# Half-height score operands replaced by zero-padded 128-row operands in the gated cell, the block attention and the sparse branches

## Chip, cores and metric

The kernel runs on 1 core of one Trainium2 chip. The metric is the device time of one execution in microseconds. TensorE is called PE here, VectorE DVE, ScalarE ACT and GpSimd POOL.

## The reference

Two transformer blocks for one sequence of 256 tokens with a width of 1024, all in float32. What matters for this change are the places in which heads of 64 channels meet in a product:

```
# gated cell (4 heads of 64): q.k weighted by exp(decays), chunkwise
w = exp(dlog - m_t) * einsum('bhtd,bhsd->bhts', q, k)
# block attention (4 heads of 64; one block of 256 keys here), relative bias, causal
s_own = einsum('bhqd,bhkd->bhqk', qc, k_own) * 64**-0.5 + bias
# sparse branches (8 query heads of 64, 2 key groups, rotary): compressed keys (15),
# selected keys and window keys; with 256 tokens all 256 keys are seen in the last two
out = g_cmp * attend(q, k_cmp) + g_slc * attend(q, k_slc) + g_win * attend(q, k_win)
```

Between and after them stand a recurrent cell with 64-channel decays, cross attention with 128-channel heads, two feed-forward parts, a forgetting attention and a table of 16384 experts.

## The kernel before

All weights come from DRAM as 450 pieces of 512 KB, through four buffers (SP issues the loads). ACT rounds each piece to a high half (`round_piece`, line 1143), DVE makes the low half (`remainder`, line 1575), and PE multiplies them as three products (`mm3`, lines 535, 538 and 539). `feed(key)` on ACT and DVE prepares the pieces of the slot after `key`. Results in the ring of four PSUM banks are ordered by one list, `jobs()`: each job waits until the job four before it has been copied out.

The products of this change are not split in halves. They are float32 matmuls, and one of them shows as two MATMUL rows in the trace. Three places have them.

The gated cell (`mlstm_unit`, units 0 to 2). Each unit makes the decays with a selector of 4 rows (`mD`, line 789) and the query-key products with 64 rows (`mQK`, line 797). Heads 0 and 2 lie in partitions 0 to 63 of their tiles, heads 1 and 3 in partitions 64 to 127. Between the first half's heads and the second half's, `fence(ins)` lets PE wait until its own last matmul is complete. Unit 0 runs before input slot 12, and units 1 and 2 between slots 12 and 13.

The block attention (`ATT1`, 3 units) makes its scores in `score(u)`, line 684, in the same manner, with a fence in each unit, among the projections of the memory.

The last attention (`ATT3`, 22 units) has 6 units of forgetting attention (line 688, whole tiles of 128 rows, whose other half holds zeros and the decays), then 4 units over compressed keys, 6 over selected keys and 6 over window keys (line 696, 64 rows: heads 0 to 3 use partitions 0 to 63, heads 4 to 7 partitions 64 to 127, so that all heads of a unit use the same half, without a fence). An iteration of `attention` on PE is: scores of unit i, in most iterations one half of a merge projection (`merge_half`, lines 535, 538, 539 into `acc`), the transposes of unit i-1 (`turn`, line 705), and the value products of unit i-2 (`pv`, line 730; those of the compressed units have 15 rows).

Around them, ACT copies the projections with their bias into SBUF (`input_copy`, lines 1243 and 1244), and DVE turns the queries and keys of the sparse branches by their rotary angles (`roped`, lines 1921 to 1923). POOL waits until the first feed-forward part is done, clears halves of the forgetting attention's tile (lines 1510 and 1511), and puts the decays in (lines 1519 to 1528).

Of the kernel before, what the change touches and what calls it, by code (L numbers as in the profile page):

```python
# [18 lines left out]
P = 128  # L19
T = 256  # L20
# [246 lines left out]
def build(nc, a):  # L267

    with ExitStack() as ctx:
# [84 lines left out]
        t1 = pl.take(18 * T).rearrange("p (k t) -> p k t", k=18)  # L354
        TT = {name: t1[:, 2 * i:2 * i + 2, :] for i, (name, _) in enumerate(T1)}
# [13 lines left out]
        hm = pl.take(NT * GW).rearrange("p (t n) -> p t n", t=NT)  # L369
        ho = pl.take(NT * GW).rearrange("p (t n) -> p t n", t=NT)  # L370
# [21 lines left out]
        nqT, kkT = t2[:, 0:4], t2[:, 4:6]  # L392
# [112 lines left out]
        def _(pe):  # L505
# [164 lines left out]
            def score(u):  # L670
# [6 lines left out]
                for i in EVEN_ODD[len(heads)]:  # L677
                    h = heads[i]
                    if i == 1 and kind == "moba":
                        fence(ins)  # L680
                    o = b[:, i * n:(i + 1) * n]
                    r = slice((h % 2) * HD, (h % 2) * HD + HD)
                    if kind == "moba":
                        ins = mm(o, TT["aq"][r, h // 2, tok], TT["ak"][r, h // 2, 0:n], start=True, stop=True)
                    elif kind == "cross":
                        ins = mm(o, cqT[:, h, tok], ckT[:, h, :], start=True, stop=True)
                    elif kind == "fox":
                        ins = mm(o, fox[:, 0, h, tok], fox[:, 1, h, 0:n], start=True, stop=True)
                    else:
                        g, hp = h // 4, h % 4  # L690
                        r = slice(g * HD, g * HD + HD)
                        if kind == "cmp":
                            k = ckc[r, 2, g * NCMP:(g + 1) * NCMP]
                        else:
                            k = kkT[r, 0 if kind == "slc" else 1, 0:n]
                        ins = mm(o, nqT[r, hp, tok], k, start=True, stop=True)
# [86 lines left out]
            def mlstm_unit(u):  # L783
# [4 lines left out]
                for i, h in enumerate(heads):  # L788
                    ins = mm(b[:, i * n:(i + 1) * n], sel4[0:4, h, :], gi[0:4, 6, tok], start=True, stop=True)
                done(ins, ("mD", u))  # L790
                b = bank(("mQK", u))
                for i in EVEN_ODD[len(heads)]:
                    h = heads[i]
                    if i == 1:
                        fence(ins)
                    r = slice((h % 2) * HD, (h % 2) * HD + HD)
                    ins = mm(b[:, i * n:(i + 1) * n], TT["mk"][r, h // 2, s * P:(s + 1) * P], TT["mq"][r, h // 2, tok],
                             start=True, stop=True)
# [312 lines left out]
        def _(act):  # L1111
# [126 lines left out]
            def input_copy(i):  # L1238

                name = T1[i][0]  # L1240
                b = got(act, ("T1", i)).rearrange("p (k t) -> p k t", k=2)
                func = {"hf": ACT.Sigmoid, "hq": ACT.Silu}.get(name, ACT.Identity)
# [262 lines left out]
        def _(pool):  # L1505
            G = nc.gpsimd

            pool.wait_ge(S("acc_ready"), NT * 3)
            for s in range(2):
                G.memset(foxh[HD:P, s, :, 0, :], 0.0).then_inc(S("fox_zero"), 1)  # L1510
                G.memset(foxh[0:HD, s, :, 1, :], 0.0).then_inc(S("fox_zero"), 1)
            pool.wait_ge(S("fox_zero"), 4)
# [19 lines left out]
        def _(dve):  # L1532
# [59 lines left out]
            def attention(units, u0):  # L1592
                for i in range(len(units) + 2):
# [21 lines left out]
                    if units is ATT3 and i == 0:  # L1615
                        link(tt(ckc[:, 1, 0:30], got(dve, ("crot",))[:, 0:30], K("sinc"), ALU.mult), "crot_done")
                        link(tt(ckc[:, 2, 0:30], ckc[:, 0, 0:30], K("cosc"), ALU.mult))
                        link(tt(ckc[:, 2, 0:30], ckc[:, 2, 0:30], ckc[:, 1, 0:30], ALU.add), "cmpk_ready")
# [67 lines left out]
            link(V.memset(C("rel", 0, 4)[32:33], NEG), "rel_ready")  # L1686
            link(V.tensor_copy(sel4[0:4], ident[0:4, 0:4].unsqueeze(2).to_broadcast([4, 4, P])), "sel_ready")
# [228 lines left out]
            def roped(i):  # L1916
# [6 lines left out]
                link(tt(o, o, r, ALU.add), "roped_all" if i == 2 else "dve_step")  # L1923
# [391 lines left out]
```

## Time and profile before

| what | value |
|---|---|
| median of three timed runs | 1624.32 us (1623.99 to 1625.88) |
| the profiled execution, its own time | 1627.78 us |
| its span in the trace | 1626.0 us |
| PE busy | 1518.1 us, 93% |
| DVE busy | 1178.9 us, 73% |
| ACT busy | 818.5 us, 50% |
| POOL busy | 15.9 us, 1% |
| mean granted PE clock | 0.970 of full speed |

Busy time counts matmuls from start to a modelled end, and they overlap, so starts of successive rows tell more than the durations. PEclk is the granted clock as a share of 2.4 GHz. "Idle before" is the time that an engine stood still before a row, with what ended it.

### The profile page before, as it was taken

How to read it: one execution, taken by the hardware profiler on the slowest of the kernel's cores; microseconds unless marked ns; L12 is line 12 of the kernel's file. 1: busy time of each engine (PE TensorE's matmuls, PEld its weight loads, DVE VectorE, ACT ScalarE, POOL GpSimd, SP SyncE). 2: the span in 40 equal slices, each digit the busy share in tenths (PEclk: the TensorE clock that was granted, in tenths of full speed). 3: DMA queues.
4: the chain of work that ended last, by engine and by line, in shares of the span. 5: the costliest groups of instructions: out<-in, count | busy, mean ns of one | idle time of the engine just before them, and what ended most of it. 6: DMA issues, size and time to landing. Idle time of an engine off the chain costs nothing.

```text
span 1626.0 us, 30064 instructions
## 1 busy us (share of the span) xinstructions
PE 1518.1 (93%) x10194; PEld 1393.9 (86%) x10194; DVE 1178.9 (73%) x2186; ACT 818.5 (50%) x1218; POOL 15.9 (1%) x16
## 2 busy tenths in 40 slices
PE   6899877899989999988999999999989999999997
PEld 5788866899869999868999998999978888889996
DVE  4666664788655575655389989989879999986665
ACT  6443555544446466545476676554533333334443
POOL 0000000000012000000000000000000000000000
PEclk9998989999998999889999999999999999999999
DMA  6443333455553541244466666443467777766553
GB/s 261 107 154 110 104 117 103 134 185 184 199 167 121 189 131 58 75 155 156 156 199 224 202 215 205 154 142 125 149 205 241 241 241 241 241 209 200 187 182 128
DMA packets 97486, 276.40 MB, mean 170 GB/s; under 512 B 10756, under 2 KB 37252, under 8 KB 96900
## 3 DMA queue, kind: packets, MB, share of 16 engines
q1 hardware_dynamic: 65808, 240.92, 45.8%
q10 hardware_dynamic: 31604, 34.49, 6.4%
q8 instruction: 48, 0.79, 0.2%
q14 instruction: 26, 0.21, 0.0%
HBM read 259.11 MB, written 16.25 MB: 169 GB/s over the span
## 4 chain that ended last, share of the span: by engine, by line
PE 80%; DVE 9%; ACT 5%; issue 3%; DMA 2%; ACTq 1%; DVEq 0%; SPq 0%
PE acc L1081 7%; PE acc L1084 7%; PE acc L1085 7%; PE ring L535 6%; PE ring L538 6%; PE ring L539 6%; PE acc L1003 4%; PE acc L1007 4%; PE acc L1008 4%; PE acc L535 4%; PE ring L1045 4%; PE acc L539 3%; PE acc L538 3%; DVE sb_halves L1575 2%; PE ring L1068 2%
## 5 line engine op out<-in xcount | busy, mean ns | idle before, releaser
L1575 DVE TENSOR_TENSOR sb_halves<-sb_raw,sb_halves 128x1024 fp32r<-128x1024 f32 x450 | 546.7, 1228 | 223.4 <-ACT sb_halves L1143 205.6
L1143 ACT ACTIVATE sb_halves<-sb_raw 128x1024 fp32r<-128x1024 f32 x450 | 469.7, 1057 | 388.7 <-PE acc L1081 166.5
L1003 PE MATMUL acc<-sb_XH,sb_halves 128*128 128x256 f32 x800 | 235.0, 294 | 7.9 <-DVE sb_halves L1575 7.1
L535 PE MATMUL ring<-sb_XH,sb_halves 128*128 128x256 f32 x784 | 224.4, 286 | 7.5 <-DVE sb_halves L1575 7.5
L1008 PE MATMUL acc<-sb_XH,sb_halves 128*128 128x256 f32 x800 | 226.5, 283 | 0.0
L1007 PE MATMUL acc<-sb_XL,sb_halves 128*128 128x256 f32 x800 | 226.5, 283 | 0.0
L538 PE MATMUL ring<-sb_XL,sb_halves 128*128 128x256 f32 x784 | 223.5, 285 | 0.0
L539 PE MATMUL ring<-sb_XH,sb_halves 128*128 128x256 f32 x784 | 223.2, 285 | 0.0
L1081 PE MATMUL acc<-sb_halves,sb_coefh 128*128 128x512 f32 x512 | 200.5, 392 | 6.8 <-DVE sb_coefl L2083 6.8
L1084 PE MATMUL acc<-sb_halves,sb_coefh 128*128 128x512 f32 x512 | 200.2, 391 | 0.0
L1085 PE MATMUL acc<-sb_halves,sb_coefl 128*128 128x512 f32 x512 | 199.7, 390 | 0.0
L1003 PEld LDWEIGHTS acc<-sb_XH,sb_halves 128*128 128x128 f32 x800 | 153.4, 192 | 12.0 <-issue 10.4
L535 PEld LDWEIGHTS ring<-sb_XH,sb_halves 128*128 128x128 f32 x784 | 152.1, 194 | 9.8 <-issue 9.4
L1007 PEld LDWEIGHTS acc<-sb_XL,sb_halves 128*128 128x128 f32 x800 | 153.7, 192 | 0.0
L1008 PEld LDWEIGHTS acc<-sb_XH,sb_halves 128*128 128x128 f32 x800 | 153.4, 192 | 0.0
L539 PEld LDWEIGHTS ring<-sb_XH,sb_halves 128*128 128x128 f32 x784 | 152.2, 194 | 0.0
L538 PEld LDWEIGHTS ring<-sb_XL,sb_halves 128*128 128x128 f32 x784 | 152.1, 194 | 0.0
L1081 PEld LDWEIGHTS acc<-sb_halves,sb_coefh 128*128 128x128 f32 x512 | 96.6, 189 | 26.8 <-issue 7.3
L1085 PEld LDWEIGHTS acc<-sb_halves,sb_coefl 128*128 128x128 f32 x512 | 96.6, 189 | 20.2
L1084 PEld LDWEIGHTS acc<-sb_halves,sb_coefh 128*128 128x128 f32 x512 | 96.7, 189 | 19.0
L2077 DVE TENSOR_TENSOR sb_area<-sb_area 128x256 f32<-128x256 f32 x126 | 78.0, 619 | 31.9 <-ACT sb_area L1457 31.9
L535 PE MATMUL acc<-sb_halves,sb_XH 128*128 128x256 f32 (+1 forms) x240 | 85.5, 356 | 9.8 <-DVE sb_XL L1568 5.9
(324 smaller groups left out, 2553.8 us busy)
## 6 DMA issues: line engine op xcount, KB each, us to landing
sb_raw<-wstream SPq DMA_DIRECT2D x450, 512.0 KB, 3.6
ahead<-sb_early ACTq DMA_DIRECT2D x100, 128.0 KB, 2.4
sb_area<-ahead ACTq DMA_DIRECT2D x98, 128.0 KB, 3.4
sb_area<-gains ACTq DMA_DIRECT2D x4, 512.0 KB, 5.1
sb_area<-consts SPq DMA_DIRECT2D x1, 1782.0 KB, 16.7
sb_area<-mem ACTq DMA_DIRECT2D x1, 1024.0 KB, 11.6
relvec<-sb_area ACTq DMA_DIRECT2D x1, 1024.0 KB
sb_area<-keys ACTq DMA_DIRECT2D x1, 1024.0 KB, 4.7
```

The source lines that it names most:

```text
L535: ins = mm(out, w[0], x[0], start=first, stop=False)
L538: mm(out, w[0], x[1], start=False, stop=False)
L539: return mm(out, w[1], x[0], start=False, stop=last)
L1003: ins = mm(o, w[0], XH[:, c, :], start=c == 0, stop=False)
L1007: mm(o, w[0], XL[:, c, :], start=False, stop=False)
L1008: ins = mm(o, w[1], XH[:, c, :], start=False, stop=c == KC - 1)
L1081: ins = mm(o, ch[:, b % 2, tok], v[0], start=start, stop=False, skip_group_check=not start)
L1084: mm(o, ch[:, b % 2, tok], v[1], start=False, stop=False, skip_group_check=True)
L1085: ins = mm(o, cl[:, b % 2, tok], v[0], start=False, stop=stop)
L1143: A(hi[:, r, :], raw[:, r, :], ACT.Copy).then_inc(S("hi_ready"), 1)
L1575: tt(lo[:, r, :], raw[:, r, :], hi[:, r, :].bitcast(F32), ALU.subtract).then_inc(S("lo_ready"), 1)
L2077: tt(g, g, table[:, :, bass.ds(n if column is None else column, 1)].rearrange("p t o -> p (t o)"), ALU.mult).then_inc(S("ex_step"), 1)
```

## The change

Every product of 64 or 4 rows in the three places is made with 128 rows. The keys get a tile for each head (or key group) whose other half is zero, and the queries are read as whole 128-row chunks, so that the second half of the query meets zeros. The three fences of the gated cell and the three of the block attention are gone. Those of the recurrent cell (lines 771 and 823) stay.

- `akz` and `mkz`: 4 heads x 256 columns each; `mkz` shares the space of `hm` and `ho`. `input_copy` on ACT writes them for slots 3 and 5 with four half-height copies where two whole ones stood, and waits once for POOL's zeros.
- `sel4` and row 6 of `gi` are cleared in all 128 partitions, and the decay product reads them whole.
- `kkz`: 2 groups x 2 kinds x 256 columns. The last step of `roped(2)` on DVE writes it as two half-height additions where one whole one stood. The compressed keys are written likewise (two small additions for one).
- POOL gets six memsets at the start of the kernel and three between its memsets and copies for the forgetting attention.

```diff
-                    if i == 1 and kind == "moba":
-                        fence(ins)
...
-                        ins = mm(o, TT["aq"][r, h // 2, tok], TT["ak"][r, h // 2, 0:n], start=True, stop=True)
+                        ins = mm(o, TT["aq"][:, h // 2, tok], akz[:, h, 0:n], start=True, stop=True)
...
-                            k = ckc[r, 2, g * NCMP:(g + 1) * NCMP]
+                            k = ckc[:, 2, g * NCMP:(g + 1) * NCMP]
...
-                            k = kkT[r, 0 if kind == "slc" else 1, 0:n]
-                        ins = mm(o, nqT[r, hp, tok], k, start=True, stop=True)
+                            k = kkz[:, g, 0 if kind == "slc" else 1, 0:n]
+                        ins = mm(o, nqT[:, hp, tok], k, start=True, stop=True)
...
-                    ins = mm(b[:, i * n:(i + 1) * n], sel4[0:4, h, :], gi[0:4, 6, tok], start=True, stop=True)
+                    ins = mm(b[:, i * n:(i + 1) * n], sel4[:, h, :], gi[:, 6, tok], start=True, stop=True)
...
-                    if i == 1:
-                        fence(ins)
-                    r = slice((h % 2) * HD, (h % 2) * HD + HD)
-                    ins = mm(b[:, i * n:(i + 1) * n], TT["mk"][r, h // 2, s * P:(s + 1) * P], TT["mq"][r, h // 2, tok],
+                    ins = mm(b[:, i * n:(i + 1) * n], mkz[:, h, s * P:(s + 1) * P], TT["mq"][:, h // 2, tok],
...
+                if name in ("mk", "ak"):
+                    if i == 3:
+                        act.wait_ge(S("pad_zero"), 4)
+                    for h in range(4):
+                        r = slice((h % 2) * HD, (h % 2) * HD + HD)
+                        ins = A((mkz if name == "mk" else akz)[r, h, :], b[r, h // 2, :], ACT.Identity,
+                                bias=C("b1", 2 * i + h // 2)[r])
+                    link(ins, "t1_copied")
+                    return
...
+            link(G.memset(sel4, 0.0), "row_zero")
+            link(G.memset(gi[:, 6, :], 0.0), "row_zero")
+            for z in (mkz, akz):
+                ze = z.rearrange("p (c e) t -> p c e t", e=2)
+                link(G.memset(ze[HD:P, :, 0, :], 0.0), "pad_zero")
+                link(G.memset(ze[0:HD, :, 1, :], 0.0), "pad_zero")
             pool.wait_ge(S("acc_ready"), NT * 3)
...
+            link(G.memset(kkz[HD:P, 0], 0.0), "key_zero")
+            link(G.memset(kkz[0:HD, 1], 0.0), "key_zero")
+            link(G.memset(ckc[:, 2, :], 0.0), "key_zero")
...
-                        link(tt(ckc[:, 2, 0:30], ckc[:, 0, 0:30], K("cosc"), ALU.mult))
-                        link(tt(ckc[:, 2, 0:30], ckc[:, 2, 0:30], ckc[:, 1, 0:30], ALU.add), "cmpk_ready")
+                        link(tt(ckc[:, 0, 0:30], ckc[:, 0, 0:30], K("cosc"), ALU.mult))
+                        for g in range(2):
+                            at, c = slice(g * HD, g * HD + HD), slice(g * NCMP, (g + 1) * NCMP)
+                            ins = tt(ckc[at, 2, c], ckc[at, 0, c], ckc[at, 1, c], ALU.add)
+                        link(ins, "cmpk_ready")
...
+            dve.wait_ge(S("row_zero"), 2)
             link(V.tensor_copy(sel4[0:4], ident[0:4, 0:4].unsqueeze(2).to_broadcast([4, 4, P])), "sel_ready")
...
-                link(tt(o, o, r, ALU.add), "roped_all" if i == 2 else "dve_step")
+                if i < 2:
+                    link(tt(o, o, r, ALU.add))
+                else:
+                    dve.wait_ge(S("key_zero"), 3)
+                    for g in range(2):
+                        at = slice(g * HD, g * HD + HD)
+                        ins = tt(kkz[at, g], o[at], r[at], ALU.add)
+                    link(ins, "roped_all")
```

## Rows read from the trace of the kernel before

**Rows 1.** The page's parts 1 and 2: span, PE's line.

```profile
span 1626.0 us, 30064 instructions
...
PE 1518.1 (93%) x10194; PEld 1393.9 (86%) x10194; DVE 1178.9 (73%) x2186; ACT 818.5 (50%) x1218; POOL 15.9 (1%) x16
```

**Rows 2.** The chain that ended last, 584 to 677 us: shares by line.

```profile
by line: PE ring L730 18.2%; PE ring L696 17.8%; PE acc L535 17.4%; PE acc L538 15.1%; PE acc L539 15.0%; PE ring L705 10.1%; PE ring L688 5.9%; PE ring L953 0.4%; PE ring L950 0.3%; PE ring L945 0.1%
```

**Rows 3.** Timeline of PE, 128-row scores: start us, us, engine, line, operation.

```profile
588.89 1.05 PE L688 MATMUL ring<-sb_area 128*128 128x128 f32 x8
...
589.90 0.28 PE L538 MATMUL acc<-sb_halves,sb_XH 128*128 128x256 f32 x1
...
604.73 1.00 PE L730 MATMUL ring<-sb_area 128*128 128x64 f32 x8
605.57 1.08 PE L688 MATMUL ring<-sb_area 128*128 128x256 f32 x4
606.49 0.60 PE L705 MATMUL ring<-sb_fixc,sb_area 128*128 128x128 f32 x4
606.92 0.45 PE L730 MATMUL ring<-sb_area 128*128 128x64 f32 x3
```

**Rows 4.** Timeline of PE, 64-row scores of the sparse branches.

```profile
657.55 1.16 PE L696 MATMUL ring<-sb_area 64*128 64x128 f32 x8
...
658.86 0.28 PE L538 MATMUL acc<-sb_halves,sb_XH 128*128 128x256 f32 x1
...
640.83 1.00 PE L730 MATMUL ring<-sb_area 128*128 128x64 f32 x8
641.76 1.13 PE L696 MATMUL ring<-sb_area 64*128 64x256 f32 x4
642.82 0.66 PE L705 MATMUL ring<-sb_fixc,sb_area 128*128 128x128 f32 x4
643.31 0.33 PE L730 MATMUL ring<-sb_area 128*128 128x64 f32 x2
```

**Rows 5.** Timeline of PE, the gated cell's units 0, 1 and 2.

```profile
130.68 2.09 PE L797 MATMUL ring<-sb_area 64*128 64x256 f32 x4 [1.76 <-DVE sb_area L1770]
132.69 0.58 PE L535 MATMUL ring<-sb_halves,sb_XH 128*128 128x256 f32 x1
...
140.93 1.13 PE L789 MATMUL ring<-sb_area 4*128 4x256 f32 x4
...
143.37 1.15 PE L789 MATMUL ring<-sb_area 4*128 4x128 f32 x8
...
146.59 0.58 PE L535 MATMUL ring<-sb_halves,sb_XH 128*128 128x256 f32 x1
```

**Rows 6.** Timeline of PE, after the block attention's second unit.

```profile
174.57 0.36 PE L535 MATMUL ring<-sb_XH,sb_halves 128*128 128x256 f32 x1 [2.26 <-DVE sb_halves L1575]
```

**Rows 7.** Timeline of ACT, after the copies of input slot 5.

```profile
77.85 0.47 ACT L1244 ACTIVATE sb_area<-ring,sb_cols 128x256 f32<-128x256 f32 x1
83.19 1.06 ACT L1143 ACTIVATE sb_halves<-sb_raw 128x1024 fp32r<-128x1024 f32 x1 [4.87 <-issue]
```

**Rows 8.** Timeline of DVE, at and after the last rotary step.

```profile
580.50 0.69 DVE L1923 TENSOR_TENSOR sb_area<-sb_area 128x512 f32<-128x512 f32 x1
...
585.44 0.69 DVE L1613 SCALAR_TENSOR_TENSOR sb_area<-ring,sb_area 128x512 f32<-128x512 f32 x1 [1.86 <-PE ring L688]
```

**Rows 9.** Timeline of POOL, one of its four memsets and its first decay copy.

```profile
481.59 0.95 POOL L1510 MEMSET sb_area<- 64x1024 f32 x1 [481.13 <-PE acc L539]
...
512.76 1.03 POOL L1525 COPY sb_area<-sb_area 8x1024 f32<-8x1024 f32 x1 [21.86 <-DVE sb_area L1895]
```

**Rows 10.** Windows: stretch and length in us, busy time by engine, PEclk, DMA share, GB/s.

```profile
620.00:630.00 10.00, 10.00 (x69) 9.16 (x67) 3.23 (x12) 5.72 (x20) 0.00 (x0) 0.83 0.08 28
140.00:150.00 10.00, 9.88 (x49) 7.98 (x48) 7.10 (x12) 3.26 (x4) 0.00 (x0) 0.74 0.01 2
584.00:677.00 93.00, 93.00 (x706) 86.65 (x705) 57.92 (x123) 58.81 (x169) 0.00 (x0) 0.98 0.26 81
```

More of the change, by code:

```diff
@@ L353, in build @@
         yc = pl.take(2 * T).rearrange("p (c t) -> p c t", c=2)
-        t1 = pl.take(18 * T).rearrange("p (k t) -> p k t", k=18)
-        TT = {name: t1[:, 2 * i:2 * i + 2, :] for i, (name, _) in enumerate(T1)}
+        t1 = pl.take(14 * T).rearrange("p (k t) -> p k t", k=14)
+        akz = pl.take(4 * T).rearrange("p (h t) -> p h t", h=4)
+        TT = {name: t1[:, 2 * i:2 * i + 2, :]
+              for i, name in enumerate(name for name, _ in T1 if name not in ("mk", "ak"))}
         v1 = pl.take(NT * 4 * 65).rearrange("p (t h d) -> p t h d", t=NT, h=4)
@@ L368, in build @@
         EW, WT = ml[:, 0:2], ml[:, 2:5]
-        hm = pl.take(NT * GW).rearrange("p (t n) -> p t n", t=NT)
-        ho = pl.take(NT * GW).rearrange("p (t n) -> p t n", t=NT)
+        hmo = pl.take(2 * NT * GW)
+        hm, ho = (hmo[:, k * NT * GW:(k + 1) * NT * GW].rearrange("p (t n) -> p t n", t=NT) for k in range(2))
+        mkz = hmo.rearrange("p (h t) -> p h t", h=4)
         hgD = pl.take(1024).rearrange("p (b n) -> p b n", b=2)
@@ L391, in build @@
         t2 = pl.take(6 * T).rearrange("p (k t) -> p k t", k=6)
-        nqT, kkT = t2[:, 0:4], t2[:, 4:6]
+        nqT = t2[:, 0:4]
+        kkz = pl.take(4 * T).rearrange("p (g k t) -> p g k t", g=2, k=2)
         kc2 = pl.take(4 * T).rearrange("p (j g t) -> p j g t", j=2, g=2)
@@ L690, in score @@
                         g, hp = h // 4, h % 4
-                        r = slice(g * HD, g * HD + HD)
                         if kind == "cmp":
-                            k = ckc[r, 2, g * NCMP:(g + 1) * NCMP]
+                            k = ckc[:, 2, g * NCMP:(g + 1) * NCMP]
                         else:
-                            k = kkT[r, 0 if kind == "slc" else 1, 0:n]
-                        ins = mm(o, nqT[r, hp, tok], k, start=True, stop=True)
+                            k = kkz[:, g, 0 if kind == "slc" else 1, 0:n]
+                        ins = mm(o, nqT[:, hp, tok], k, start=True, stop=True)
                 done(ins, ("score", u))
@@ L793, in mlstm_unit @@
                     h = heads[i]
-                    if i == 1:
-                        fence(ins)
-                    r = slice((h % 2) * HD, (h % 2) * HD + HD)
-                    ins = mm(b[:, i * n:(i + 1) * n], TT["mk"][r, h // 2, s * P:(s + 1) * P], TT["mq"][r, h // 2, tok],
+                    ins = mm(b[:, i * n:(i + 1) * n], mkz[:, h, s * P:(s + 1) * P], TT["mq"][:, h // 2, tok],
                              start=True, stop=True)
@@ L1506, in _ @@
             G = nc.gpsimd
+            link = stepper(pool, "pool_step")
+            link(G.memset(sel4, 0.0), "row_zero")
[4 more added lines that the diff above has]
+                link(G.memset(ze[0:HD, :, 1, :], 0.0), "pad_zero")
             pool.wait_ge(S("acc_ready"), NT * 3)
```

## The prediction

> **What bounds the kernel now.** I read the page first: PE is busy 93% of a span of 1626.0 us, and no other engine comes near it [rows 1]. So PE's time is worth most, but only where PE itself ends the waits. The changed products stand in three stages, and each has to be read by itself. The chain that ended last tells which stage is PE's. From 584 to 677 us, where all 22 units of the last attention have their scores, every share of the chain is a PE line [rows 2]: whatever PE loses there is lost in full. Then I read PE's timeline by the starts of its rows, because the durations overlap. In the gated cell the units 1 and 2 follow the projection of slot 12 without an idle gap, and unit 0 waits 1.76 us for DVE before its query-key products and then runs on into slot 12 [rows 5]. In the block attention PE stands still 2.26 us after unit 1, until DVE delivers the low half of a weight piece [rows 6]: that stage belongs to ACT and DVE.
>
> **The last attention, per unit.** The forgetting attention makes scores of the same sizes with 128 rows, so it is the measure of what a unit costs after the change. With four heads of 128 keys it takes from 588.89 to the second projection row at 589.90, 1.01 us [rows 3]; the 64-row unit takes from 657.55 to 658.86, 1.31 us [rows 4]. The difference is 0.30 us, without the border in front of the unit. With two heads of 256 keys I compare whole rounds between value products: 604.73 to 606.92 is 2.19 us with 128 rows [rows 3], and 640.83 to 643.31 is 2.48 us with 64 rows [rows 4]. The difference of 0.29 us splits into 0.09 before the scores (641.76 less 640.83 against 605.57 less 604.73), 0.14 behind them and 0.06 at the transposes. So the 64 rows cost nothing in the products themselves, and about 0.29 us per unit goes at the two borders between 64-row and 128-row work. There are 16 such units: eight with two heads of 256 keys, four with four heads of 128, and the four compressed ones, whose 15 keys have no 128-row counterpart and for which I take the same. 16 x 0.29 = 4.64 us. In four of them (the last compressed one and the first three over selected keys) the row before the scores is a 15-row value product, so there the border in front stays: 4 x 0.09 = 0.36 us less. This stage gives **4.3 us**. The lower bound is the part behind the scores alone (0.14 and 0.06), 16 x 0.20 = 3.2, and the upper 0.39 (0.30 and the 0.09 in front) in eight units with 0.29 in the other eight, 5.4 us.
>
> The Trainium skill has the cause: "TensorEngine Tiling (Array Packing)", section "Key Properties", says that a change of the tiling mode drains the engine. For a size there is "TensorE: Matmul & The Clock Gate", section "Step-by-step: what each phase is for", which puts the drain of the array at about 128 cycles. An estimate from that page is 128 / 2.4 GHz = 0.05 us a border, so 28 borders (16 x 2 less 4) would give 1.5 us, and the sum below 3.5 instead of 6.3. The rows measure 0.29 us for two borders, and I go by them.
>
> **The gated cell.** Unit 1 takes from 140.93 to 143.37, 2.44 us, for eight rows of 256 columns [rows 5]. The forgetting attention takes 0.92 us for four (605.57 to 606.49) [rows 3], hence 1.84 for eight, and 0.60 us goes: the fence and the borders. Unit 2 takes 3.22 us (143.37 to 146.59) for sixteen rows of 128 columns. At full clock 16 would be 1.6 to 1.8 us, but the clock was granted at 0.74 in this stretch [rows 10], so a part of the 3.22 is a slow clock and stays. I take 0.8 us, between the 0.6 of unit 1 and the 1.5 of a full clock. Unit 0's query-key products take 2.01 us to the first row of slot 12, also partly at half clock; four rows need 0.92 at full and some 1.7 at half clock, so 0.3 to 1.1 us goes, and I take 0.7. Its decay product now has a border in front (it follows 4-row transposes) of 0.1 us, on the way through DVE to the same spot. Sum: 0.6 + 0.8 + 0.7 - 0.1 = **2.0 us**, bounds 1.4 and 3.1. Behind it stand slot 13 and PE transposes, without a wait for DMA, so it carries through.
>
> **The block attention.** The three fences and six borders go, about 3 x 0.5 us of PE, but PE then waits longer for the low halves (2.26 us already) [rows 6]. I take 0, with 1.5 us as the other bound.
>
> **What is added.** ACT gets four extra copies, two each in slots 3 and 5. A copy takes 0.47 us [rows 7], so a slot has at most 0.94 us more; ACT then stands idle 4.87 us [rows 7], and after slot 3 the gap is larger. Cost 0; without that cover the next piece would be rounded 0.94 us late, and PE would wait as long. DVE's last rotary step becomes two additions, 0.69 us more at 580.50 [rows 8]. Queued behind it are the two low halves of a merge slot and then the first scores, for which DVE stands idle 1.86 us; so it had done all that at 583.6 (585.44 less 1.86) and 0.69 us fits; PE has the first scores and the products of the compressed keys ahead of the next merge projection. The one small addition more for the compressed keys is hidden by the next wait of DVE. POOL clears 64x1024 in 0.95 us [rows 9]. The six memsets at the start are of half that size or less, some 3 us in all, long before DVE and ACT ask for them. The three new ones before the copies of the forgetting attention take 1.2 us and move four copies back by as much; the next thing POOL does comes 21.86 us later [rows 9]. DVE's wait for the zeros, at the last rotary step near 580 us, is met about 90 us before. DMAs are not touched. Cost of all: 0, at most 0.7 us if one of the covers is thinner than read.
>
> **Sum.** 4.3 + 2.0 + 0 = 6.3 us. The profiled execution took 1627.78 us (its span is 1626.0), 3.5 above the median of the three runs; the same change there would give 1621.5. Against the median of 1624.32 it gives **1618.0 us**.
>
> **Rivals.**
> 1. *The borders stay.* The 0.29 us may belong to other things, such as the reading of another tile, and only the fences go. Then only the gated cell's fences give something, at most half of its 2.0 us: 1623.3. Against it: the borders are there in both sizes, on both sides, and not in the forgetting attention, which reads the same memory. Chance 0.10.
> 2. *A hand-over to ACT takes the place.* PE's value products need attT, which ACT copies after two roundings. If PE runs 0.3 to 0.5 us earlier per round, it may wait for that copy in the three or four rounds that have no merge half. At 0.5 us each that is 2 us back: 1620.0. In this stretch ACT is busy for 58.81 of 93 us [rows 10], which speaks against a longer queue. Chance 0.10.
> 3. *The fences of the block attention count too.* 1.5 us more: 1616.5. Against it stands the idle 2.26 us. Chance 0.06.
> 4. *The clock is granted for less time: slower.* The same waits with less PE work between them make PE idler in the gated cell and beside the compressed units, just where the clock already fell, to 0.83 in 620 to 630 us and 0.74 in 140 to 150 [rows 10]. A stretch like the first costs 10 x 0.17 = 1.7 us. To turn the forecast into 0.2% slower it must cost 6.3 + 3.2 = 9.5 us, that is more than five such stretches more. PE is busy for all of the 93 us of the last attention [rows 10], so I see room for one or two (1620 to 1621), not six (1628). Chance of ending slower 0.05.
> 5. *Halves that ran side by side are now serial.* Heads 2 and 1 of a unit lie in different halves. If they overlapped before, padding would lose up to 0.9 us in each of the three units of the gated cell: 1618.0 + 2.7 = 1620.7. But a fence stood between them, and all heads of a sparse unit use one half. Chance 0.03. The Trainium skill, "TensorE: Matmul & The Clock Gate", section "Part 3: Packing small matmuls — row/col tiling", recommends just this: keep small products in different row groups so that they run concurrently; by it the change would be in the wrong direction. The rows do not show overlap to lose: eight 64-row rows start as far apart as eight 128-row ones, save at the borders.
>
> **How the numbers follow.** My forecast has 0.66, the rivals 0.10, 0.10, 0.06, 0.05 and 0.03. What can be told from no change here is 0.2%, 3.25 us: below 1621.1 is faster. Rival 1 and the weak tail of the forecast with the clock's rival are "same" (0.10 + about 0.06), rival 4 slower, the rest faster: 0.79, 0.16 and 0.05. The range: the bounds of the parts are 3.2 + 1.4 - 0.7 = 3.9 and 5.4 + 3.1 + 1.5 = 10.0 us (1620.4 and 1614.3), and one stretch of half clock, 1.7 us, can go either way. 1613.5 to 1622.5 holds the forecast but for its outer tails and rivals 2, 3 and 5, and leaves out rivals 1 and 4 (0.15).
>
> **What would show it.** In the changed trace the scores of a sparse unit with 256 keys should go from value products to value products in about 2.2 us instead of 2.48; the stretch from the first to the last score of the last attention, 584 to 677 us before, should be some 4.3 us shorter. Unit 1 of the gated cell should take about 1.85 us and slot 13 start some 2.0 us earlier against slot 4's start. PE's idle before line 535 at 174 us should grow, not vanish. ACT's gap after slot 5 should shrink from 4.87 to about 4 us with no PE wait behind it. The prediction would be wrong if PE shows new waits before line 730, if the rounds stay at 2.48 us, or if the granted clock is below 0.97 by 0.005 or more.

## The result and the profile after

The changed kernel takes 1611.97 us (median of four runs, 1611.01 to 1612.92) against 1624.59 us for the kernel before, run beside it: a ratio of 0.9923 with an interval of 0.9908 to 0.9937, or 12.6 us faster. The forecast was 6.3 us and its range ended at 1613.5, so the sign was right and half of the gain was not foreseen. The profiled execution took 1611.59 us. The page of the kernel after, parts 1 and 2, to be read against [rows 1]:

```profile
span 1609.7 us, 30083 instructions
...
PE 1503.8 (93%) x10194; PEld 1387.9 (86%) x10194; DVE 1179.6 (73%) x2188; ACT 820.8 (51%) x1222; POOL 19.8 (1%) x25
```

PE issues as many rows as before and is busy for 14.3 us less, while DVE and ACT changed by 0.7 and 2.3 us. To find where, I cut both traces at the same instructions: from unit 0's query-key products in the gated cell to the transposes behind slot 13, and a stretch of the last attention that holds all 16 changed units and ends a few rows into its last value products. Windows of the kernel before (columns as in [rows 10]; the last but two is PEclk):

```profile
130.68:154.63 23.95, 23.77 (x124) 20.71 (x125) 13.55 (x23) 4.84 (x6) 0.00 (x0) 0.71 0.28 89
...
599.84:681.95 82.11, 80.70 (x602) 74.38 (x601) 51.42 (x115) 48.98 (x142) 0.00 (x0) 0.97 0.24 78
```

Windows of the kernel after:

```profile
130.70:146.95 16.25, 16.25 (x124) 15.77 (x125) 13.56 (x23) 4.86 (x6) 0.00 (x0) 1.00 0.23 72
...
590.70:667.50 76.80, 75.03 (x602) 71.89 (x601) 51.42 (x115) 48.85 (x142) 0.00 (x0) 1.00 0.25 83
```

The counts are equal, so the same work is compared. The gated stretch lost 7.7 us (2.0 forecast) and the last attention 5.3 (4.3 forecast), together 13.0 of the 16.3 us between the two spans. In both the granted clock rose to 1.00, from 0.71 and 0.97. The column of the clock holds what the forecast lacks.

The window of the last attention stops before that attention is over. Timeline of PE at its end, before:

```profile
680.22 0.67 PE L705 MATMUL ring<-sb_fixc,sb_area 128*128 128x128 f32 x4 [1.41 <-ACT sb_area L1186]
...
685.28 3.67 PE L666 MATMUL ring<-sb_fixc,sb_area 128*128 128x128 f32 x16 [0.78 <-DVE sb_area L1651]
```

and after:

```profile
666.29 0.63 PE L705 MATMUL ring<-sb_fixc,sb_area 128*128 128x128 f32 x4 [1.74 <-ACT sb_area L1183]
...
670.19 3.67 PE L670 MATMUL ring<-sb_fixc,sb_area 128*128 128x128 f32 x16 [0.78 <-DVE sb_area L1670]
```

From the first compressed scores (607.86 before, 598.63 after) to the transposes that follow the attention (line 666 before, 670 after) it is 77.42 us before and 71.56 after, so the whole last attention gave 5.9 us. PE waits 0.33 us longer for ACT before its last transposes.

The gated cell row by row, timeline of PE in the kernel after, against [rows 5]:

```profile
130.70 1.13 PE L794 MATMUL ring<-sb_area 128*128 128x256 f32 x4 [1.76 <-DVE sb_area L1790]
131.48 0.47 PE L539 MATMUL ring<-sb_halves,sb_XH 128*128 128x256 f32 x1
...
137.43 1.03 PE L789 MATMUL ring<-sb_area 128*128 128x256 f32 x4
...
139.15 1.05 PE L789 MATMUL ring<-sb_area 128*128 128x128 f32 x8
...
141.10 0.38 PE L539 MATMUL ring<-sb_halves,sb_XH 128*128 128x256 f32 x1
...
146.95 1.91 PE L559 MATMUL ring<-sb_fixc,sb_area 128*128 128x128 f32 x16
```

Unit 0's products take 0.78 us (2.01 before), unit 1 takes 1.72 (2.44), unit 2 takes 1.95 (3.22). That is 3.2 us. The other 4.5 us come from slots 12 and 13, whose own products did not change: 131.48 to 137.43 is 5.95 us against 8.24 (132.69 to 140.93), and 141.10 to 146.95 is 5.85 against 8.05 (146.59 to 154.64).

The last attention, timeline of PE in the kernel after, against [rows 4]:

```profile
628.93 1.00 PE L730 MATMUL ring<-sb_area 128*128 128x64 f32 x8
...
631.14 1.07 PE L730 MATMUL ring<-sb_area 128*128 128x64 f32 x8
...
644.67 1.11 PE L696 MATMUL ring<-sb_area 128*128 128x128 f32 x8
...
645.75 0.28 PE L542 MATMUL acc<-sb_halves,sb_XH 128*128 128x256 f32 x1
```

A round with 256 keys is 2.21 us (2.48 before, 2.2 forecast), and a unit with four heads of 128 keys 1.08 (1.31).

### The profile page after: what moved, and what is told of

It is laid out like the page before. It is cut to its first block, busy times and chain, and to the rows that moved or that the text cites. A ratio compares the mean times of both kernels' runs of the same rounds, so it can differ in the third digit from the quotient of the medians.

```text
span 1609.7 us, 30083 instructions
## 1 busy us (share of the span) xinstructions
PE 1503.8 (93%) x10194; PEld 1387.9 (86%) x10194; DVE 1179.6 (73%) x2188; ACT 820.8 (51%) x1222; POOL 19.8 (1%) x25
## 3 DMA queue, kind: packets, MB, share of 16 engines
HBM read 259.11 MB, written 16.25 MB: 171 GB/s over the span
## 4 chain that ended last, share of the span: by engine, by line
PE 80%; DVE 9%; ACT 5%; issue 3%; DMA 2%; ACTq 0%; DVEq 0%; SPq 0%
PE acc L1078 7%; PE acc L1081 7%; PE acc L1082 7%; PE ring L539 6%; PE ring L542 6%; PE ring L543 6%; PE acc L1000 5%; PE acc L1004 4%; PE acc L1005 4%; PE ring L1042 4%; PE acc L539 3%; PE acc L542 3%; PE acc L543 3%; DVE sb_halves L1591 2%; PE ring L1065 2%
```

## The experiments

All edits are against the kernel before or after, as named; the ratio is to the kernel before in the same set of runs, whose medians were 1625.7, 1625.39, 1625.26 and 1625.29 us.

**The changed kernel again**, to see how its stages vary.

> The changed kernel, profiled and timed a second time. Theory A: about 1612 us again, no half clock between 128 and 150 us. Theory B: the falls move about from one profile to the next; the time stays near 1612 (it is a median of four), but the stage looks otherwise.

1612.67 us, 0.992 (0.9905 to 0.9935). Two lines of this profile matter, the window of the gated stretch and PE's timeline at the block attention:

```profile
129.44:147.02 17.58, 17.58 (x125) 17.01 (x125) 13.56 (x23) 4.85 (x6) 0.00 (x0) 0.90 0.23 69
```

```profile
166.95 0.45 PE L539 MATMUL ring<-sb_XH,sb_halves 128*128 128x256 f32 x1 [3.43 <-DVE sb_halves L1591]
```

The gated stretch is 17.6 us here; the window of the last attention repeated to 0.01 us. The six kernels with extra products further down are this kernel up to 630 us, so they show the same stage six times more: with both profiles here, the gated stretch is 16.3 us at a clock of 1.00 in three of eight and 17.6 at 0.90 in five.

**The kernel before again**, unedited, one profile.

> The kernel before, profiled a second time, to see which stretches at half clock belong to the kernel and which to the one execution. Theory A (the half-height and 4-row products of the gated cell bring the clock down): the fall near 131 us and near 145 us, and the one beside the compressed units, come again at about the same places, and slot 12 and 13 are again partly at half clock. Theory B (chance of the one profile): the falls of that stage are elsewhere or missing, and the span is nearer to 1622 us.

1621.8 us. Windows of the same two stretches:

```profile
130.26:152.04 21.78, 21.61 (x125) 18.55 (x126) 13.57 (x23) 4.85 (x6) 0.00 (x0) 0.81 0.29 90
...
597.21:679.32 82.11, 80.70 (x601) 74.38 (x601) 51.47 (x115) 49.02 (x142) 0.00 (x0) 0.97 0.24 78
```

Over two profiles of each kernel the gated stretch is 22.9 us before (23.95 and 21.78) and 16.9 after (16.25 and 17.58), so 6.0 us shorter. Two of the kernels below keep the old stage (23.93 and 24.02 us); over these four profiles and the eight with the changed stage it is 23.4 against 17.1, 6.4 us shorter. The window of the last attention is 82.11 both times before and 76.8 both times after.

**Only the sparse branches padded** (before, with `kkz`, the full `ckc[:, 2]`, their memsets and additions).

```diff
-                            k = kkT[r, 0 if kind == "slc" else 1, 0:n]
-                        ins = mm(o, nqT[r, hp, tok], k, start=True, stop=True)
+                            k = kkz[:, g, 0 if kind == "slc" else 1, 0:n]
+                        ins = mm(o, nqT[:, hp, tok], k, start=True, stop=True)
```

> The kernel before with only the sparse branches padded (keys of the compressed, selected and window units, whole query chunks). By my sum 4.3 us of borders: 1620.2. If a fall of the clock beside the compressed units goes too, 1.7 us more: 1618.5. If nearly all of the 12.6 us comes from here, 1613.

1618.16 us, 0.9956 (0.9942 to 0.9969). Windows, gated stretch and last attention:

```profile
129.24:153.17 23.93, 23.75 (x124) 20.39 (x125) 13.56 (x23) 4.94 (x6) 0.00 (x0) 0.72 0.28 89
...
598.14:674.95 76.81, 75.03 (x601) 71.89 (x601) 51.48 (x115) 48.78 (x142) 0.00 (x0) 1.00 0.26 83
```

**Only the gated cell padded** (before, with `mkz`, `sel4` and `gi` over 128 rows, its fences gone).

```diff
-                    ins = mm(b[:, i * n:(i + 1) * n], sel4[0:4, h, :], gi[0:4, 6, tok], start=True, stop=True)
+                    ins = mm(b[:, i * n:(i + 1) * n], sel4[:, h, :], gi[:, 6, tok], start=True, stop=True)
-                    ins = mm(b[:, i * n:(i + 1) * n], TT["mk"][r, h // 2, s * P:(s + 1) * P], TT["mq"][r, h // 2, tok],
+                    ins = mm(b[:, i * n:(i + 1) * n], mkz[:, h, s * P:(s + 1) * P], TT["mq"][:, h // 2, tok],
```

> The kernel before with only the gated cell padded, decay and query-key products, its three fences gone. My forecast for this part was 2.0 us. If the half-height products also bring the clock down in this stage, it is some 6 us below before (about 1619), and the stretch from unit 0's products to the end of slot 13 falls from 22.2 (mean of the three profiles with the old stage) to 16 to 17 us.

1618.25 us, 0.9953 (0.9941 to 0.9965). Windows:

```profile
130.41:146.68 16.27, 16.27 (x125) 15.77 (x126) 13.58 (x23) 4.85 (x6) 0.00 (x0) 1.00 0.23 72
...
594.26:676.51 82.25, 80.84 (x602) 74.73 (x601) 51.47 (x115) 48.99 (x142) 0.00 (x0) 0.97 0.23 78
```

These two runs are a cross: each stretch gets its shorter time and its clock of 1.00 where its own operands are padded, and keeps 0.72 or 0.97 where they are not. Within these two stretches the clock therefore follows the change in the stretch itself and not something earlier in the kernel. The two medians give 7.5 and 7.1 us; their sum, 14.6, is more than the 13.0 of the whole change, a difference that intervals of 2 us each don't resolve. The expectation took 22.2 us for the mean of three old profiles; the three give 23.2.

Behind the gated stretch this is not so. The block attention's part, from the transposes behind slot 13 to the projection row behind unit 1, shows as a window, here with its old operands:

```profile
146.68:170.43 23.75, 22.35 (x126) 20.51 (x124) 16.03 (x40) 15.63 (x35) 0.00 (x0) 0.71 0.18 56
```

and in the changed kernel's first profile:

```profile
146.95:167.89 20.94, 19.66 (x127) 19.24 (x125) 13.80 (x37) 15.51 (x35) 0.00 (x0) 0.76 0.13 48
```

Before, the same part took 19.93 us (154.64 to 174.57) at a clock of 1.00. So a fall of the clock that left the gated stretch came back in the part behind it, 3.8 us of the 7.7 were lost again in this profile, and the two parts together are 40.0 us against 43.9 before and 37.2 in the changed kernel.

**Only the decays, only the query-key products of the gated cell**: the one or the other pair of lines of the diff above.

> The kernel before with only the decay products padded (selector and decay row, 4 rows to 128); query-key products with 64 rows and fences as before. Theory clock-by-height: 4-row products count least, so this alone brings back a good part of the clock: 2 to 4 us below before, less half clock in slots 12 and 13. Theory fences: nothing but borders, which now stand between decay and query-key products instead: within 0.5 us of before.

> The kernel before with only the query-key products of the gated cell padded and its three fences gone; the decay products keep 4 rows. With both padded it was 7.1 us below before, with the decays alone 1.9. If the parts add, this is 5 us below before (about 1620.4), and half clock in slots 12 and 13 shrinks from some 11 us to 0 to 5. If the 4-row products are enough to bring the clock down, it is 1.5 to 2.5 us below before with the half clock still there.

Decays 1623.5 us, 0.9988 (0.9979 to 0.9998); products with their fences gone 1619.66, 0.9968 (0.9958 to 0.9979). Window of the gated stretch, decays alone:

```profile
129.35:150.21 20.86, 20.68 (x124) 17.77 (x125) 13.57 (x23) 4.85 (x6) 0.00 (x0) 0.84 0.24 75
```

and products alone:

```profile
130.26:148.58 18.32, 18.32 (x125) 17.00 (x126) 13.55 (x23) 4.84 (x6) 0.00 (x0) 0.91 0.23 71
```

With one profile each, the decays alone (20.9 us, 0.84) are a little below the lowest of the four old ones (21.8, 0.81), and the products alone show the clock that both together have in five of eight profiles (0.91 and 0.90). The 64-row products weigh more than the 4-row ones; what the 4-row ones do to the clock is within the spread. With the products alone the part behind the gated stretch shows what the block attention's fences and borders cost:

```profile
148.58:170.80 22.22, 20.82 (x127) 18.98 (x125) 14.87 (x39) 15.63 (x35) 0.00 (x0) 0.77 0.11 39
```

That is 22.22 us with the old operands and 20.94 with the padded ones, at the same clock and with no wait of PE at the end of either: 1.3 us.

**Only the compressed keys padded**, the 15-key units.

```diff
-                            k = ckc[r, 2, g * NCMP:(g + 1) * NCMP]
+                            r = slice(0, P)
+                            k = ckc[:, 2, g * NCMP:(g + 1) * NCMP]
```

> The kernel before with only the four compressed units padded (their keys, 15 columns a head); selected and window units still with 64 rows. Borders: 4 x 0.29 less what stays beside 64-row and 15-row work, about 0.9 us. If the fall of the clock to a half that follows these units in each profile of the old stage comes from their 64-row products, it is gone and gives 1.7 us more: 2.6 us in all, with no half clock between 600 and 640 us. If the fall comes from the 15-row value products or from shortness alone, it stays: 0.9 us.

1623.58 us, 0.9986 (0.9977 to 0.9995), 1.8 us by the medians. Window of the last attention:

```profile
599.21:679.99 80.78, 79.37 (x601) 73.27 (x601) 51.47 (x115) 48.77 (x142) 0.00 (x0) 0.98 0.25 79
```

The four compressed units give 1.3 us of the 5.3, and the clock still falls. The fall that stood between 622 and 627 us before stands between 628 and 633 us now, among the selected units, which still have 64 rows here.

**The six fences put back** (after, padded operands).

```diff
+                    if i == 1:
+                        fence(ins)
```

> The changed kernel with all six fences put back (three in the gated cell, three in the block attention) and the padding kept. If the fences are what costs the time in the gated cell (0.3 us each and an idle PE that brings the clock down), it is 1614 to 1618 us. If the height of the products is what matters for borders and clock, it is 1612.5 to 1613.5: only three fences of 0.25 us on the way.

1615.0 us, 0.993 (0.9916 to 0.9944), against 1612.67 for the changed kernel in the same set: 2.3 us of the 13.0 hang on the fences. Window of the gated stretch:

```profile
129.46:147.94 18.48, 18.31 (x125) 16.66 (x126) 13.57 (x23) 4.85 (x6) 0.00 (x0) 0.91 0.25 74
```

The gated stretch is 0.9 us longer than in the changed kernel's second profile (17.58) at the same clock: three fences, 0.3 us each. The padding alone brings the clock from 0.71 and 0.81 to 0.91, and the window of the last attention, where no fence stands, is 76.81 us at 1.00 as in the changed kernel. So rival 1 (only the fences count) is out in both stretches. But 1615.0 us lies in the range that the expectation gave to the fences (1614 to 1618), not in the one for the height alone: six fences at 0.3 us would be 1.8 us, and in this profile the part behind the gated stretch took 21.53 us (147.94 to 169.47) with the clock down in it, against 19.93 in the changed kernel's second profile, whose gated clock is the same. Whether the fences brought that fall is open, since it also stands in three of eight profiles without them.

**A dense row of extra products.** Why did the clock fall? I put 48 products of 256 keys ahead of one unit over selected keys of the changed kernel, once with 64 and once with 128 rows, and then alternating. The output is not used. These six kernels have one profile each.

```diff
+                if kind == "slc" and t == 1 and heads[0] == 4:
+                    for k in range(48):
+                        ins = mm(b[:, 0:n], nqT[0:64, k % 4, tok], kkz[0:64, 0, 0, 0:n], start=True, stop=True)
```

> The changed kernel with 48 extra products ahead of the scores of one selected unit, 64 rows each, 256 columns, all in the lower half of the array, without a wait or a border between them; their result is overwritten. At full clock they take 48 x 0.43 = 20.6 us. Theory clock-by-height: although PE has no gap, the granted clock falls to a half during or right after the run, and it takes up to 41 us. Theory clock-by-gaps: the clock stays at full, about 1633 us in all.

> The same with 128 rows in the extra products. Both theories: the clock stays at full, 20.6 us more than the changed kernel, about 1633 us. If the clock falls here too, float32 products as such bring it down, whatever their height, and the theory of height is wrong.

> After, with 48 extra products of 256 keys ahead of one unit over selected keys, as in the two probes before it (20.5 us for 48 at either height), but here the heights alternate: 64 rows, 128 rows, 64 rows, and so on, which makes 47 borders between the extra products. If a border costs what two of them cost around a unit of the last attention (0.29 us, so 0.145 each), the 48 take 20.5 + 47 x 0.145 = 27.3 us. An estimate by the Trainium skill, 'TensorE: Matmul & The Clock Gate', section 'Step-by-step: what each phase is for' (a drain of about 128 cycles), is 0.05 us a border and 22.9 us. If the price around the units belongs to something else than the change of height, 20.5 us. If borders themselves bring the granted clock down, it falls below 1.00 in this stretch, which it did not with either height alone.

Timeline of PE, 64 rows:

```profile
637.26 20.98 PE L683 MATMUL ring<-sb_area 64*128 64x256 f32 x96
658.17 1.13 PE L699 MATMUL ring<-sb_area 128*128 128x256 f32 x4
```

128 rows:

```profile
633.58 20.94 PE L683 MATMUL ring<-sb_area 128*128 128x256 f32 x96
654.36 1.03 PE L699 MATMUL ring<-sb_area 128*128 128x256 f32 x4
```

Alternating, and a window inside it:

```profile
632.37 30.19 PE L684 MATMUL ring<-sb_area 64*128 64x256 f32 x96
662.39 1.03 PE L700 MATMUL ring<-sb_area 128*128 128x256 f32 x4
```

```profile
640.00:650.00 10.00, 10.00 (x33) 4.69 (x33) 0.00 (x0) 0.00 (x0) 0.00 (x0) 1.00 0.00 0
```

Height alone costs nothing: 20.91 us against 20.78. Alternating takes 30.02 us, 9.24 more than 128 rows for 48 borders (the one in front included), so **0.19 us a border**. That is above the 0.145 of the forecast and far above its estimate of 0.05; the change of height is the cause, as the same products in the same place show. The clock stayed at 1.00 in all three, so neither long half-height products nor borders lower it by themselves. The window teaches something else: PE reads "busy" for 10.00 of 10 us while a third of the time goes at borders. Only the count (33 rows, where the 64-row probe had 48) tells.

**The same with short products**: 96 products of 64 columns.

```diff
+                    for k in range(96):
+                        q = 64 + 64 * (k % 2)
+                        ins = mm(b[:, 0:64], nqT[0:q, k % 4, tok], kkz[0:q, 0, 0, 0:64], start=True, stop=True)
```

> After, with 96 extra products of 64 keys and 64 rows at the same place. Each is a quarter as long as those of the probe before, so borders and loads weigh more. A value product of 128 rows and 64 columns starts 0.105 us after the one before it, two rows to a product, so 96 products take about 20 us. If short products of half height are what brings the granted clock down in the gated cell and the compressed units, it falls here; if height and length in a dense row leave it alone, it stays at 1.00.

> As the probe with 96 short products of 64 rows, but with 128 rows. Both theories: about 20 us at a granted clock of 1.00. It is the measure for the other two: if a product of 64 rows were cheaper when it is short (its load is of half the size), this one would be longer.

> As the probe with 96 short products, heights alternating between 64 and 128 rows: 95 borders. At 0.145 us each 13.8 us more than with one height, some 34 us; by the estimate of 0.05 us 4.8 us more. If borders with short work between them bring the granted clock down, this is the run where it must fall, to 0.5 for part of the stretch; if it stays at 1.00 the falls of the kernel before in the gated cell and the last attention come from something else, such as gaps.

64 rows, timeline of PE and two windows:

```profile
632.06 36.43 PE L684 MATMUL ring<-sb_area 64*128 64x64 f32 x192
668.42 2.07 PE L700 MATMUL ring<-sb_area 128*128 128x256 f32 x4
```

```profile
632.00:637.00 5.00, 5.00 (x46) 4.94 (x45) 1.48 (x5) 1.69 (x5) 0.00 (x0) 1.00 0.01 3
...
640.00:650.00 10.00, 10.00 (x49) 10.00 (x48) 0.00 (x0) 0.00 (x0) 0.00 (x0) 0.50 0.00 0
```

128 rows:

```profile
637.30 21.60 PE L684 MATMUL ring<-sb_area 128*128 128x64 f32 x192
658.74 1.08 PE L700 MATMUL ring<-sb_area 128*128 128x256 f32 x4
```

```profile
640.00:650.00 10.00, 10.00 (x92) 10.00 (x92) 0.00 (x0) 0.00 (x0) 0.00 (x0) 1.00 0.00 0
```

This shows one way in which the clock is lost. Back to back, short products of 64 rows run at 1.00 for some five us and at 0.50 from then on, and take 36.4 us; with 128 rows, at the same length and count, they run at 1.00 throughout and take 21.4. The upper 64 rows of the keys hold only zeros, and they keep the clock. Neither row has a gap in which PE waits. For the kernel itself it is support and not proof: the gated cell's 64-row products have 128 and 256 columns, the compressed ones 15, and no run here tried 64 rows with 128 columns in a dense row. What the kernel's own stages show is the cross above.

Alternating short products took 55.3 us (632.84 to 688.15), and fell to 0.50 as well, though every second one has 128 rows. Timeline of PE in its part at 1.00, and in a part at 0.50:

```profile
632.84 4.43 PE L684 MATMUL ring<-sb_area 64*128 64x64 f32 x24
```

```profile
639.57 10.55 PE L684 MATMUL ring<-sb_area 128*128 128x64 f32 x34
```

By the starts of the rows a product takes 0.36 us here at full clock and 0.62 at half; with one height it takes 0.22 and 0.43. So a border between short products is 0.14 us at full clock and 0.19 at half.

**The recurrent cell's levels padded too** (after, a further step). The levels' products, `64*128` with 128 columns, are the short half-height products that remain. ACT copies each level's keys into a zeroed tile.

```diff
+                A(hgZe[0:HD, :, 0, :], src[0:HD], ACT.Copy)
+                link(A(hgZe[HD:P, :, 1, :], src[HD:P], ACT.Copy), "hg_z")
```

> The changed kernel with the recurrent cell padded in the same manner: ACT copies each level's factors into a tile for each head whose other half is zero, the queries are read whole, and the eighteen fences of lines 771 and 823 (before) are gone. A level takes 2.30 us for 16 rows on PE; 16 rows of 128 want 1.7, and two borders go. Eight levels and the last product at 0.6 to 0.8 us are 5 to 7 us, if PE stays the engine that ends the waits from 69 to 126 us: about 1606. ACT gets two copies of half height per level, 1.2 us; if it becomes the bound or delays the pieces, 1610 to 1613.

> As the kernel with the recurrent cell padded too, but POOL makes the two half-height copies of each level instead of ACT, so that they don't queue behind ACT's wait for a late weight piece. The level stage was 5.7 us shorter with ACT's copies, and the start 6.8 us longer by that wait. If the wait was the cause, the start is back at 54.9 us to slot 4 and the time near 1606.5 us. If POOL's copies are slow (over 2 us a level) or hold up DVE, PE waits before the levels and it is 1608 to 1612.

> After, with the keys of the recurrent cell's levels padded too and copied by ACT, but each level's pair of copies stands ahead of ACT's roundings of the next weight piece instead of behind them. Before, that stage became 5.7 us shorter and the start in front of it 6.8 us longer, since the first pair waited with ACT for a piece that the DMA queue delivered late (PE waited 8.7 us for the copy). If that order alone was the loss, the pair is done some 7 us earlier, the start is back at 55 us, and the kernel ends at 1607 to 1609, 4 to 6 us faster than after. Rival: the roundings behind the copies now come 1.3 us late each time (and wait with them for DVE's scaled keys), the low halves of DVE and PE's projections with them, and nothing is left: 1612 to 1615.

> As the version above, but only the first pair of copies, the one that met the late piece, stands ahead of the roundings; the others stay behind them. If the late piece was the whole loss it gives the same 1607 to 1609 and is free of the rival's delay; if this gains and the other doesn't, the delay of the roundings is real. If neither gains, the 6.8 us at the start has another cause than the order on ACT: then 1612 to 1613.

Copies by ACT 1612.98 us, 0.9922 (0.9909 to 0.9936); by POOL 1612.84, 0.9927 (0.9914 to 0.9941); by ACT ahead of the weight pieces 1616.9, 0.9945 (0.9933 to 0.9957); the first pair alone ahead 1615.58, 0.9941 (0.9927 to 0.9955). None beats the changed kernel. The waits of PE from 10 to 130 us say why (line and what it waited for, total, times, longest). In the changed kernel they come to 6.0 us (the two below and one of 0.2), besides two of 13.2 and 3.0 us that all have in like size:

```profile
PE ring L539 <- DVE sb_halves L1591: 4.3, 3, 2.3
...
PE ring L778 <- DVE sb_area L1770: 1.5, 1, 1.5
```

Copies by ACT (and 2.4 us of other waits):

```profile
PE ring L777 <- ACT sb_area L1262: 10.1, 2, 8.7
```

Copies by POOL, the wait, and two of the copies in POOL's timeline:

```profile
PE ring L777 <- POOL sb_area L1525: 7.5, 4, 2.9
```

```profile
64.42 0.61 POOL L1525 COPY sb_area<-sb_area 64x512 f32<-64x512 f32 x1
74.38 1.60 POOL L1524 COPY sb_area<-sb_area 64x512 f32<-64x512 f32 x1 [9.34 <-DVE sb_area L1776]
```

Copies ahead of the pieces:

```profile
PE ring L777 <- ACT sb_area L1262: 4.8, 3, 2.8
```

With 3.8 and 3.2 us behind DVE that is 11.8 us. The wait of 8.7 us did go when the first pair was moved, but the total stayed between 11 and 13 us in all three orders on ACT: the copy stands between DVE's scaled keys and PE, and whatever it gives PE in speed PE then waits for. Unit 0 of the gated cell starts at 135.15 us with the copies ahead, against 130.70 in the changed kernel. My theory that the order on ACT was the whole loss fell.

## Why the prediction had the sign and only half of the size

**The last attention (4.3 us, measured 5.3 in the window and 5.9 to its end).** The borders hold and the rounds came out nearly as forecast: 0.27 us instead of 0.29 for 256 keys, 0.23 instead of 0.30 for 128, 0.22 to 0.25 for the first three compressed units, and 0.1 to 0.2 where a 15-row product keeps the border in front. The 16 units make about 3.6 us. The round that held the fall of the clock between 622 and 627 us, from value products to value products, took 7.02 us before (620.05 to 627.07) and 5.42 after (610.22 to 615.64): 1.5 us of it is clock, near the 1.7 that [rows 10] gives, and it is gone. At the end the last value products ran wholly at half clock before (3.65 us) and partly after (2.49), 1.2 us less, of which the longer wait for ACT took 0.3 back. The term was too large by 0.7 in its borders and had nothing for the clock, which gave some 2.7 us.

**The gated cell (2.0 us, measured 7.7 in the profile and 6.4 over all).** Here is the failed step: "a part of the 3.22 is a slow clock and stays". It did not stay: unit 2 went from 3.22 to 1.95 us. The fences and borders give some 1.6 us: before, the clock of 0.71 means 13.9 us at half speed, and slot 12 shows what such time costs (2.3 us longer for 5.3 us at half clock, 0.44), so some 6.1 of the 7.7 are clock. I read the 0.74 in [rows 10] as a condition of that stretch, while it went with the very products that the change removes, and it also slowed slots 12 and 13, to which I gave nothing and which gave 4.5 us.

**Rival 4 had the right quantity and, in the two changed stretches, the wrong sign.** I took less PE work as a reason for a lower clock. The crossed runs and the short probes show the reverse there: half-height work lowered it, padded work restores it. Padding did not end the falls: in five of eight profiles the gated stretch still has one, and in the other three it stands in the part behind, among products that all have 128 rows, as rival 4 feared. What brings those falls is open. Over the whole span the granted clock rose from 0.970 and 0.969 only to 0.973 and 0.972, about 10 us less at half clock and so, at 0.44 each, some 4.6 of the 12.6 us at most. Some of the falls that left the two stretches came back where PE had a wait to absorb them.

**The block attention (0 us) was right where PE still waits**, as in five of eight profiles. Its sign is in the changed kernel's second one: PE stands 3.43 us before line 539 where it stood 2.26, and the time from the transposes behind slot 13 to that row is 19.93 us in both (147.02 to 166.95, and 154.64 to 174.57). What the fences and borders gave, PE waited. In the first profile after, the clock fell between 153 and 163 us instead, the idle was gone, and the same stretch took 20.94 us (146.95 to 167.89). There the fences and borders do count: the 1.3 us against 22.22 are what rival 3 priced at 1.5. Either way the gated stretch and this part together take 37.2 to 37.5 us, in all eight profiles, against 43.9 in three of the four old ones and 41.7 in the other: 6.0 us by the means. No run changed the block attention alone.

**The added work (0 us) was right.** ACT's gap after slot 5 went from 4.87 to 3.47 us, 1.4 us less where 0.9 was forecast. Timeline of ACT after, against [rows 7]:

```profile
82.27 1.06 ACT L1140 ACTIVATE sb_halves<-sb_raw 128x1024 fp32r<-128x1024 f32 x1 [3.47 <-issue]
```

DVE's two additions took their 0.69 us out of its idle of 1.86 before the first scores, which is 1.16 now. Timeline of DVE after, against [rows 8]:

```profile
576.30 0.69 DVE L1629 SCALAR_TENSOR_TENSOR sb_area<-ring,sb_area 128x512 f32<-128x512 f32 x1 [1.16 <-PE ring L689]
```

Rival 2 came only once: PE's wait for ACT before the last transposes grew from 1.41 to 1.74 us, and no other round got longer. Rival 5 (halves that ran side by side) is out by the units themselves, since unit 1, at full clock in both kernels, went from 2.44 to 1.72 us; the extra products used one half only and don't test it.

**The balance.** The gated stretch with the part behind it gives 6.0 us and the whole last attention 5.9, together 11.9 of a median gain of 12.6. The forecast had 2.0 and 4.3. The rest lies in other stages, where single falls of the clock move about between profiles of one kernel; it is not settled.

## What to carry to other kernels

Where a stretch shows a granted clock below 1.00, ask which of its products use half the rows and are short before taking the clock as given: padding them with zeros cost nothing on PE here and gave back most of the clock for the unchanged work beside them. Then see whether the fall has only moved into the next stage, and measure both stages together. Count 0.14 us (64 columns) to 0.19 us (256 columns) for each border between products of 64 and 128 rows at full clock. Padding pays where the zeros are written once and the data go straight into the padded tile; where every use needs a copy between its maker and PE, the wait ate the gain in each of the four versions.

## What the runs showed of the hardware

- Short products of 64 rows (64 columns, back to back) were granted 0.50 of the clock, 1.2 GHz, after some five us at 1.00, in a row in which PE never waited; with 128 rows, half of the keys' zeros, 1.00 for all 21.4 us. With 256 columns 64 rows had 1.00 for all 20.9 us. Alternating 64 and 128 rows with 64 columns fell to 0.50 too. The Trainium skill, "TensorE: Matmul & The Clock Gate", section "HAM oscillation — how this bites in real kernels", speaks of gaps in which PE is idle; here the clock was lost without one, and the measurement decides.
- A border took 0.19 us between products of 256 columns at full clock, and 0.14 at full and 0.19 at half clock between products of 64 columns. The Trainium skill, the same page, section "Single matmul latency", says of a single bf16 matmul that the drain takes roughly 175 ns whatever the clock. The borders of this case lie on both sides of that figure, and no run here shows that a border is such a drain. The estimate of 0.05 us from the 128 cycles of another section does not price a border.
- POOL's copy of 64x512 took 0.61 us with DVE idle and 1.60 beside DVE's making of a low half. The Trainium skill, "SBUF — State Buffer", section "🔬 SBUF: two separate sides", says that DVE and POOL lock a pair of ports against each other; the rows are what that would give, and no run here separates it from other causes.
